# Strassen weight sums made by adding transfers from GpSimd and two negated copies by ScalarE, in place of four VectorE additions

## The reference, cut to what matters

```python
D_MODEL = 1024
D_FF = 2816
...
def swiglu(h, w1, w2):
    g, u = jnp.split(h @ w1, 2, axis=-1)
    return (jax.nn.silu(g) * u) @ w2
...
        hn = modulate(rmsnorm(x, norm_g[l, 0]), sh1, sc1)
        x = x + 0.5 * g1[:, None, :] * swiglu(hn, ffn_w1[l, 0], ffn_w2[l, 0])
        ...
        hn = modulate(rmsnorm(x, norm_g[l, 2]), sh3, sc3)
        x = x + 0.5 * g3[:, None, :] * swiglu(hn, ffn_w1[l, 1], ffn_w2[l, 1])
```

## Time and profile before

| | |
|---|---|
| time, median of 3 runs | 1447.94 us (1447.08 to 1450.46) |
| span of the profiled execution | 1443.5 us, 4.4 us below the median |
| TensorE matmul busy | 1422.6 us, 99% of the span, granted clock 0.998 |
| VectorE, ScalarE, GpSimd busy | 1014.8 us, 662.9 us, 71.0 us |
| HBM and DMA traffic | 161.02 MB by DMA, mean 112 GB/s |
| chain of work that ended last | TensorE 92% |

### The profile page before, as it was taken

The page is one execution under the profiler, slowest core; times in us unless marked ns, Lnnn a source line. Parts: engine busy times, 40 slices in busy tenths (PEclk is TensorE's granted clock), DMA queues, the critical chain, the costliest instruction groups (busy, mean ns, idle before and its releaser), DMA issues.

```text
span 1443.5 us, 25671 instructions
## 1 busy us (share of the span) xinstructions
PE 1422.6 (99%) x10206; PEld 1372.1 (95%) x10206; DVE 1014.8 (70%) x1742; ACT 662.9 (46%) x1186; POOL 71.0 (5%) x121
## 2 busy tenths in 40 slices
PE   7999999999999999999999999999999999999998
PEld 6899999999999999999789999998999999999997
DVE  5667667676777776667886567557767686767776
ACT  5543525253435444576825453226425253444354
POOL 4000000000000130000100000004000000000001
PEclk9999999999999999999999999999999999999999
DMA  9752534445344612231362222444324232231221
GB/s 308 206 194 65 154 115 142 122 133 160 110 139 132 183 31 74 74 93 55 98 186 77 68 73 63 132 144 122 110 58 142 67 88 89 71 106 52 81 74 74
DMA packets 219532, 161.02 MB, mean 112 GB/s; under 512 B 6826, under 2 KB 204646, under 8 KB 219426
## 3 DMA queue, kind: packets, MB, share of 16 engines
q1 hardware_dynamic: 217026, 153.87, 35.8%
q0 software_dynamic: 1696, 5.56, 1.3%
q10 hardware_dynamic: 704, 0.12, 0.0%
HBM read 151.50 MB, written 8.03 MB: 111 GB/s over the span
## 4 chain that ended last, share of the span: by engine, by line
PE 92%; DVE 2%; DMA 1%; SPq 1%; ACT 1%; POOL 1%; issue 0%; DVEq 0%; ACTq 0%
PE acc L844 25%; PE acc L1176 19%; PE pC L1067 18%; PE acc L1067 14%; PE acc L1055 4%; PE pB L966 2%; PE acc L1125 2%; PE pC L1316 1%; DMA ada_raw<-in_w_ada 1%; PE pB L925 1%; DMA raw<-in_ffn_w 1%; PE pB L1301 1%; SPq L601 1%; PE pC L1451 1%; PE pC L1335 1%
## 5 line engine op out<-in xcount | busy, mean ns | idle before, releaser
L1547 ACT ACTIVATE slot<-raw 128x512 fp32r<-128x512 f32 (+1 forms) x310 | 189.5, 616 | 238.2 <-PE acc L1176 137.8
L2122 DVE TENSOR_TENSOR slot<-raw,slot 128x512 fp32r<-128x512 f32 (+1 forms) x310 | 208.4, 676 | 54.5 <-ACT slot L1547 51.9
L1176 PE MATMUL acc<-hid_hi,slot 128*128 128x320 f32 x1240 | 238.5, 310 | 0.0
L1067 PE MATMUL pC<-hn_hi,slot 128*128 128x320 f32 x912 | 216.3, 309 | 0.0
L1176 PEld LDWEIGHTS acc<-hid_hi,slot 128*128 128x128 f32 x1240 | 195.1, 188 | 2.9 <-issue 2.5
L844 PE MATMUL acc<-hn_hi,whi 128*128 128x320 f32 x672 | 161.0, 321 | 0.0
L1067 PEld LDWEIGHTS pC<-hn_hi,slot 128*128 128x128 f32 x912 | 156.2, 188 | 2.5 <-issue 2.5
L844 PE MATMUL acc<-hn_hi,wlo 128*128 128x320 f32 x672 | 153.1, 309 | 0.0
L844 PE MATMUL acc<-hn_lo,whi 128*128 128x320 f32 x672 | 153.0, 309 | 0.0
L1067 PE MATMUL acc<-tT,slot 128*128 128x320 f32 x912 | 146.3, 309 | 0.0
L1176 PE MATMUL acc<-hid_lo,slot 128*128 128x320 f32 x620 | 142.0, 308 | 0.0
(11 more groups left out here) (389 smaller groups left out, 2407.1 us busy)
## 6 DMA issues: line engine op xcount, KB each, us to landing
raw<-in_ffn_w SPq DMA_DIRECT2D x88, 512.0 KB, 5.2
sraw<-in_w_ada SPq DMA_DIRECT2D x26, 1024.0 KB, 7.7
wraw<-in_w_in SPq DMA_DIRECT2D x36, 512.0 KB, 3.8
raw<-in_ffn_w SPq DMA_DIRECT2D x16, 1024.0 KB, 5.1
ada_raw<-in_w_ada SPq DMA_DIRECT2D x8, 1024.0 KB, 12.0
wraw<-in_w_out SPq DMA_DIRECT2D x16, 512.0 KB, 4.1
raw<-in_ffn_w SPq DMA_DIRECT2D x8, 768.0 KB, 4.4
sraw<-in_w_ada_final SPq DMA_DIRECT2D x6, 1024.0 KB, 7.4
```

The lines of the kernel that those rows point to most:

```text
L1067: last = mm(out, w[:, kk * P:(kk + 1) * P], a, start=(first and kk == 0 and t == 0), stop=(kk == KQ - 1 and t == 2), skip_group_check=not ...
L1176: last = mm(a[h], w[t // 2][:, k, :], (hid_hi, hid_lo)[t % 2][:, k * TOK + h * HALF:k * TOK + (h + 1) * HALF], start=(k == 0 and t == 0), ...
L1547: A(slot_as(fi, b, 0), source_of(fi, b), ACT.Copy).then_inc(blk_hi, 1)
L2122: V.tensor_tensor(out=slot_as(fi, b, 1), in0=source_of(fi, b), in1=slot_as(fi, b, 0).bitcast(F32), op=ALU.subtract).then_inc(blk_lo, 1)
```

## The change

- The four VectorE additions per Strassen pair (19 pairs, two FFNs) go.
- SyncE loads a21 a second time, 256 KB, into the buffer of S1 (`s1_of`: `s1w` and the first 512 columns of `xadd` in turn), on the same semaphore as the pair's job, behind its two transfers.
- GpSimd (`weight_sums`) issues four transfers SBUF to SBUF of 128x512 with an addition into the target: a22 into the copy of a21 (S1); `s2w`, which holds -a11, into a21 (this is -S3); S1 into `s2w` (S2); a12 into a11, which then holds -S2 (S4).
- ScalarE makes the two negated copies that these need: -a11 into `s2w`, in `blk` two blocks ahead of the pair's block 0; -S2 into a11, behind block 2.
- The blocks' waits are for the two new semaphores `s12_sum` and `s34_sum`. The third activation combination changes its sign, since S3 has.
- Three semaphores are merged into others: `vecs_in` into `c_in`, `c_used` into `c_silu`, and `s_sum` goes.

```diff
-                    n += 16 if q in JOB_DOWN or q - 1 in JOB_DOWN else 32
+                    n += 16 if q in JOB_DOWN or q - 1 in JOB_DOWN else 32 + 16 * int(q in JOB_PAIR[PLAIN:])
...
+    def s1_of(p):
+        return xadd[:, 0:WB] if (p - PLAIN) % 2 else s1w[:, :]
...
-        return (w[:, 0:WB], w[:, 2 * WB:3 * WB], s2w[:, :], w[:, 3 * WB:4 * WB], s1w[:, :], w[:, WB:2 * WB],
+        return (w[:, 0:WB], w[:, 2 * WB:3 * WB], s2w[:, :], w[:, 3 * WB:4 * WB], s1_of(p), w[:, WB:2 * WB],
...
-    S_AT = {1: 2, 2: 3, 4: 1, 6: 4}
+    S_AT = {1: (s34_sum, 16), 2: (s12_sum, 32), 4: (s12_sum, 16), 6: (s34_sum, 32)}
...
+                if p >= PLAIN:
+                    sp.dma_start(kxn(s1_of(p), KQ, P), w1[fi][:, 0:KQ, D_FF + p * P:D_FF + (p + 1) * P]
+                                 ).then_inc(done, 16)
...
+        def weight_sums(fi):
+
+            for p in range(PLAIN, N_PAIR):
+                n, r = wino_before(fi, p), JOB_PAIR[p]
+                w, s1 = raw[raw_of(fi, r)], s1_of(p)
+                pool.wait_ge(raw_in[raw_of(fi, r)], raw_count(fi, r))
+                pool.dma_start(s1, w[:, 3 * WB:4 * WB], accum_op=ALU.add).then_inc(s12_sum, 16)
+                pool.wait_ge(neg_ready, 2 * n + 1)
+                wait(pool, s34_sum, 32 * n)
+                pool.dma_start(w[:, 2 * WB:3 * WB], s2w[:, :], accum_op=ALU.add).then_inc(s34_sum, 16)
+                pool.wait_ge(s12_sum, 32 * n + 16)
+                pool.wait_ge(s34_sum, 32 * n + 16)
+                pool.dma_start(s2w[:, :], s1, accum_op=ALU.add).then_inc(s12_sum, 16)
+                pool.wait_ge(neg_ready, 2 * n + 2)
+                pool.dma_start(w[:, 0:WB], w[:, WB:2 * WB], accum_op=ALU.add).then_inc(s34_sum, 16)
+
...
+        weight_sums(0)
...
-                act.wait_ge(s_sum, 4 * wino_before(fi, p) + S_AT[j])
+                act.wait_ge(S_AT[j][0], 32 * wino_before(fi, p) + S_AT[j][1])
...
             A(slot_as(fi, b, 0), source_of(fi, b), ACT.Copy).then_inc(blk_hi, 1)
+            if kind == "wino" and j == 2:
+                act.wait_ge(blk_lo, fi * NB + b - 1)
+                A(raw[raw_of(fi, job_of(b))][:, 0:WB], s2w[:, :], ACT.Copy, scale=-1.0).then_inc(neg_ready, 1)
+            if b + 2 < NB and BLOCK[b + 2][0] == "wino" and BLOCK[b + 2][2] == 0:
+                r = job_of(b + 2)
+                act.wait_ge(raw_in[raw_of(fi, r)], raw_count(fi, r))
+                wait(act, neg_ready, 2 * wino_before(fi, BLOCK[b + 2][1]))
+                if BLOCK[b + 2][1] > PLAIN:
+                    act.wait_ge(blk_lo, fi * NB + BLK_PAIR[BLOCK[b + 2][1] - 1] + 3)
+                A(s2w[:, :], raw[raw_of(fi, r)][:, 0:WB], ACT.Copy, scale=-1.0).then_inc(neg_ready, 1)
...
-        def s_add(out, in0, in1, op):
-            V.tensor_tensor(out=out, in0=in0, in1=in1, op=op).then_inc(s_sum, 1)
-
-        def first_sums(fi, b):
-
-            if b not in BLOCK or BLOCK[b][0] != "wino" or BLOCK[b][2] or (fi, b) in summed:
-                return
-            summed.add((fi, b))
-            w = raw[raw_of(fi, job_of(b))]
-            a11, a21, a22 = w[:, 0:WB], w[:, 2 * WB:3 * WB], w[:, 3 * WB:4 * WB]
-            dve.wait_ge(raw_in[raw_of(fi, job_of(b))], raw_count(fi, job_of(b)))
-            n = wino_before(fi, BLOCK[b][1])
-            if n:
-                dve.wait_ge(blk_lo, last_low[4])
-            s_add(s1w[:, :], a21, a22, ALU.add)
-            dve.wait_ge(s_sum, 4 * n + 1)
-            s_add(a21, a11, a21, ALU.subtract)
-        summed, last_low = set(), {}
-
         def blk(fi, b):
...
-            if kind == "wino":
-                n = wino_before(fi, p)
-                first_sums(fi, b)
-                if j == 1:
-                    if n:
-                        dve.wait_ge(blk_lo, last_low[2])
-                    dve.wait_ge(s_sum, 4 * n + 2)
-                    s_add(s2w[:, :], s1w[:, :], w[:, 0:WB], ALU.subtract)
-                if j == 3:
-                    dve.wait_ge(s_sum, 4 * n + 3)
-                    dve.wait_ge(blk_lo, fi * NB + b - 2)
-                    s_add(w[:, 0:WB], w[:, WB:2 * WB], s2w[:, :], ALU.subtract)
             dve.wait_ge(blk_hi, fi * NB + b + 1)
...
-            V.tensor_tensor(out=half_of(t34_f(kk), 0), in0=half_of(b, 1), in1=half_of(a, 1), op=ALU.subtract)
+            V.tensor_tensor(out=half_of(t34_f(kk), 0), in0=half_of(a, 1), in1=half_of(b, 1), op=ALU.subtract)
...
             blk(fi, b + 12)
-            first_sums(fi, b + 14)
```

More of the change, by code:

```diff
@@ L234, in trunk_program @@
     c_in, setup_in, tok_sq = sem("c_in"), sem("setup_in"), sem("tok_sq")
-    vecs_in = sem("vecs_in")
     x_in = [sem(f"x_in{i}") for i in range(TT)]
@@ L239, in trunk_program @@
     c_silu = sem("c_silu")
-    c_tr, c_used, quads_done = sem("c_tr"), sem("c_used"), sem("quads_done")
+    c_tr, quads_done = sem("c_tr"), sem("quads_done")
     par_tr = sem("par_tr")
@@ L254, in trunk_program @@
     raw_in = [sem(f"raw_in{i}") for i in range(2)]
-    blk_hi, blk_lo, blk_done, s_sum = sem("blk_hi"), sem("blk_lo"), sem("blk_done"), sem("s_sum")
+    blk_hi, blk_lo, blk_done = sem("blk_hi"), sem("blk_lo"), sem("blk_done")
+    s12_sum, s34_sum, neg_ready = sem("s12_sum"), sem("s34_sum"), sem("neg_ready")
     snap, c_sum, silu_done, hidp_done, down_used = (
@@ L809, in _ @@
         norm_samples(3, None, 6 * KD, 7 * KD)
+        weight_sums(1)
         pool.wait_ge(mod_ready, 6)
@@ L949, in _ @@
         spread_r(0)
-        pe.wait_ge(c_used, 1)
+        pe.wait_ge(c_silu, 2)
         pe.wait_ge(quads_done, 2)
@@ L1660, in _ @@
         for q, src in enumerate((dt_bias, a_log, d_skip)):
-            act.dma_start(vecs[:, q, :], src[0].partition_broadcast(P)).then_inc(vecs_in, 16)
+            act.dma_start(vecs[:, q, :], src[0].partition_broadcast(P)).then_inc(c_in, 16)
         def copy_c():
@@ L1665, in copy_c @@
             c_cols = pB[:, 0:KD * NSTR].rearrange("p (k c) -> p k c", c=NSTR)
-            A(c_f32[:, :, 0:NSTR], c_cols, ACT.Copy).then_inc(c_used, 1)
+            A(c_f32[:, :, 0:NSTR], c_cols, ACT.Copy).then_inc(c_silu, 1)
         for c in range(TT):
@@ L1759, in ffn @@
                 if part == last_part and fi == 0:
-                    act.wait_ge(vecs_in, 48)
+                    act.wait_ge(c_in, 16 * (2 + 3))
                     st.done(A(vecs[:, 1, :], vecs[:, 1, :], ACT.Exp))
@@ L2106, in blk @@
                 return
-            kind, p, j = BLOCK[b]
-            w = raw[raw_of(fi, job_of(b))]
-            if kind == "wino":
-                n = wino_before(fi, p)
-                first_sums(fi, b)
-                if j == 1:
-                    if n:
-                        dve.wait_ge(blk_lo, last_low[2])
-                    dve.wait_ge(s_sum, 4 * n + 2)
-                    s_add(s2w[:, :], s1w[:, :], w[:, 0:WB], ALU.subtract)
-                if j == 3:
-                    dve.wait_ge(s_sum, 4 * n + 3)
-                    dve.wait_ge(blk_lo, fi * NB + b - 2)
-                    s_add(w[:, 0:WB], w[:, WB:2 * WB], s2w[:, :], ALU.subtract)
             dve.wait_ge(blk_hi, fi * NB + b + 1)
@@ L2123, in blk @@
                             op=ALU.subtract).then_inc(blk_lo, 1)
-            if kind == "wino":
-                last_low[j] = fi * NB + b + 1
         def add_square(k, square=sq):
```

## The result

The changed kernel takes 1512.35 us in the median of 4 runs (1508.28 to 1521.13), the kernel before 1447.51 us (1446.52 to 1450.46, 4 runs) beside it: a ratio of 1.0461 [1.0438, 1.0483], 65 us slower. Forecast were 1457 us, with a range of 1450.5 to 1480. The sign was right, the size was not.

A forecast was written before the change was run, and what follows sets the result against it. TensorE, busy 1422.6 of 1443.5 us, was taken as the bound. Ends of parts 7.9, interior 0 and leakage 1 made 9 us: 1452.5 us of span, plus 4.4 around it, 1457 us; range 1450.5 to 1480.

The forecast's parts named there:

- D: Time of one adding transfer, from its release to the waiter's start: taken as 3.5 us, free up to about 4.1.
- the 0 for the interior of a part: Inside a part, the negated copies and the -S3 and S2 transfers before block 2 were to cost TensorE 0 us.
- the prediction's own formula: Inside parts: two transfers, each D less 4.1 us, for 16 pairs in all; at D of 4.6 it gave 16 us.
- the case of slow transfers: Rival inside parts: adding transfers of 4.6 us or more, or slowed by loads; 16 us more, 1473 us; chance 0.30.
- the price of 48 us: Extreme of the slow-transfer rival: D of 5.6 us inside parts, 48 us more, about 1505 us; chance 0.05.
- I add 1 us in all for what of this leaks through.: Inside parts, loads and adding transfers share DMA engines with 2 us left for it; 1 us added in all.
- The budget of 8.6 us: Inside a part, from 1100.4 to block 2's latest start at about 1109.0: 8.6 us for two transfers, -S3 and S2.
- ends of parts: The next pair's -a11 copy waits for its load ahead of `hid_hi`; TensorE waits at ten places, 7.9 us.
- 1.2 us in two plain pairs: TensorE's longest wait inside an FFN before the change, read as 1.2 us in two plain pairs at its start.
- The third load piece: At ends of parts, the added 256 KB load: 0.85 us behind the second half, bounds 0.4 and 1.7 us.
- VectorE's relief: Removing 152 additions, 104 us of VectorE's time, was to gain 0 because TensorE had no gap behind them.
- a starved GpSimd: Rival: each GpSimd issue waits out one VectorE instruction, D 4.2 us, 3 us paid, 1460 us; no chance of its own.

The follow-up runs named there:

- both cures: Changed kernel with S2 made by a VectorE addition and, at ends of parts, the negated -a11 copy put behind `hid_hi`: 1447.49 us, ratio 1.0006.

## Why the prediction was wrong, by its own steps

- **"D ... I take 3.5 us" and the 0 for the interior of a part: the step that failed.** In place of 0 the runs show 40.1 us of snapshot waits in 17 gaps. As the price of one undisturbed adding transfer 3.5 us was good (3.3 us from issue to landing, 3.8 from release to the next issue). It was put on S2, which is hardly ever undisturbed (3 of 38). With the medians of the changed kernel, -S3 at 4.0 and S2 at 5.3 to 6.2, each with 0.5 us from its release to GpSimd's issue (the prediction took 0.2), D is 5.4 in the mean, and the prediction's own formula gives 2 x (5.4 - 4.1) x 16 = 42 us (35 if its 0.2 us for wake-ups are not taken off twice). That this comes near 40.1 is in part luck: the formula has equal waits in 16 pairs, while four of them had none and others up to 6.2 us; and with -S3 taken off the chain it gives no wait at all (S2 alone has 8.2 us), where 32.0 us were measured.
- **The collision was named and priced too low.** "The load of the next job falls on the S2 transfer in each pair" stands among the rivals, in the case of slow transfers; 0.30 went to 16 us more, and 0.05 to the price of 48 us (1505 us), which is the one near the 1512.35 measured.
- **"I add 1 us in all for what of this leaks through."** This is where the collision was waved off. It asked whether the load would come late because of the transfers. The question was the other way round: what the load does to the transfer that somebody waits for. The Trainium skill ("DMA: Bandwidth & Descriptors", Anatomy of one DMA) has a formula for one GpSimd-issued DMA, by which 256 KB take an estimated 2.6 us. It has no term for what else is in flight: the undisturbed copies are near it (2.3 to 2.5 us), the copy that mostly lay beside a load is not (`s2w<-xadd`, 5.1 us).
- **The budget of 8.6 us started from the -a11 copy's end: the path was too short.** In the trace -S3 starts at S4's landing, and S4 at the -S2 copy, so each late block 2 makes the next pair late as well. The prediction checked that S4 lands in time for its own reader and did not follow it to the next pair. Cutting this one link is worth about 7 us (1.0461 to 1.0412, intervals that just don't meet). That the rest is a ring too, through S1, is shown by the two runs with sums on VectorE.
- **No term for TensorE's clock.** Gaps were costed at their length. About 20 us more came at the 1.2 GHz level, most of it behind gaps, also at the ends of parts: 9.8 us of waits there came with 5.6 us more of busy time, 3.4 of it at the lower clock.
- **A misreading that changed nothing.** The "1.2 us in two plain pairs" is the sum of two waits, the longer 0.8 us, one in each FFN.
- **The ends of parts were right:** 7.9 us forecast in ten places, 9.0 in nine (the changed kernel) and 9.8 in ten (S2 on VectorE) measured. The third load piece was under-priced (2.0 us behind the second half at the place shown, not 0.85), but the second half came 1.2 us earlier than before, so the sum held there; in part that is luck.
- **Right as well:** VectorE's relief is worth 0 (1.0006 with both cures), a starved GpSimd didn't show (undisturbed transfers 3.3 us beside a working VectorE), and the ScalarE copies cost nothing where their sources were there (with both cures they stand in the list and TensorE doesn't wait).

The loss is thus: transfers in the ring about 40 us of waits, ends of parts 9, lower clock about 20, and about 6 us of busy time whose cause stays open. These are of the profiled execution, which lies 76 us above the one of before; the medians differ by 65.

## What to carry to other kernels

A transfer between two waits must be priced beside what else is in flight at its moment, not by the fastest row of its size: look up which load is issued while it runs. Draw the whole ring from one use of a buffer to the next and compare it with the time that the bound engine gives one turn; semaphores that merely keep a count in order are links of it too. And a gap in front of a TensorE that is otherwise always busy can cost more than its length: look at the granted clock behind it.
